# Streaming-encoder kernel: the head's transfers of x and of the first weight units in one queue, in order of use

## What is computed

```
def swiglu(x, w_gate, w_up, w_down):
    return (jax.nn.silu(x @ w_gate) * (x @ w_up)) @ w_down

for l in range(DEPTH):                       # DEPTH = 2
    h = rms_norm(x, ffn1_norm[l])
    x = x + 0.5 * swiglu(h, ffn1_w_gate[l], ffn1_w_up[l], ffn1_w_down[l])
    h = rms_norm(x, mix_norm[l])
    p = h @ w_in[l]
    ...                                      # attention, HGRN2, S5, all from p
    x = x + jnp.concatenate([o_a, o_b, o_c], axis=-1) @ w_out[l]
    h = rms_norm(x, ffn2_norm[l])
    x = x + 0.5 * swiglu(h, ffn2_w_gate[l], ffn2_w_up[l], ffn2_w_down[l])
```

## Time and profile before

| | us |
|---|---|
| median of three runs | 1030.37 |
| lowest and highest of them | 1029.40, 1030.59 |
| the profiled execution | 1029.56 |
| its span, first to last instruction | 1027.5 |
| PE busy in the span | 1014.0 (99%) |

### The profile page before, as it was taken

One profiled execution on the slowest core, in us unless ns is written; L12 is line 12 of the kernel. 1 busy time (PEld: TensorE's weight loads), 2 busy tenths in 40 slices (PEclk: granted clock), 3 DMA queues, 4 the chain that ended last, 5 costly groups with the idle time before them and its releaser, 6 DMA issues.

```text
span 1027.5 us, 20654 instructions
## 1 busy us (share of the span) xinstructions
PE 1014.0 (99%) x8562; PEld 946.8 (92%) x8562; DVE 744.4 (72%) x950; ACT 558.4 (54%) x699; POOL 199.2 (19%) x271
## 2 busy tenths in 40 slices
PE   9999999999999999999999999999999999999998
PEld 8998999999899999999999898989998998989898
DVE  7677778988778666565667777897987767666664
ACT  6656444655477645454476554446456866444442
POOL 0000899700002000000020019994000020000000
PEclk9999999999999999999999999999999999999999
DMA  8745354434325454645555455444442264554551
GB/s 302 277 151 217 151 211 157 165 127 162 125 83 205 164 209 160 209 158 210 187 193 207 173 195 202 166 147 181 142 149 84 86 243 166 204 187 181 187 180 41
DMA packets 26817, 178.39 MB, mean 174 GB/s; under 512 B 3120, under 2 KB 4160, under 8 KB 5760
## 3 DMA queue, kind: packets, MB, share of 16 engines
q1 hardware_dynamic: 25632, 173.03, 46.1%
q10 hardware_dynamic: 1008, 4.05, 1.1%
q0 software_dynamic: 112, 0.40, 0.1%
HBM read 176.42 MB, written 1.05 MB: 173 GB/s over the span
## 4 chain that ended last, share of the span: by engine, by line
PE 89%; DVE 7%; ACT 2%; issue 1%; DMA 0%; ACTq 0%; DVEq 0%
PE ps L887 23%; PE ps L835 16%; PE ps L836 16%; PE ps L837 16%; PE ps L889 12%; DVE lo L1246 2%; ACT hi L589 2%; PE ps L997 1%; PE ps L1106 1%; DVE fqk L1669 1%; PE ps L1050 1%; DMA x<-xT 0%; DVE in_lo L1484 0%; PE ps L1072 0%; DVE key L1550 0%
## 5 line engine op out<-in xcount | busy, mean ns | idle before, releaser
L887 PE MATMUL ps<-xg,hi 128*128 128x512 f32 x1120 | 397.8, 399 | 0.3
L1246 DVE TENSOR_TENSOR lo<-raw,hi 128x2048 fp32r<-128x2048 f32 x130 | 302.3, 2354 | 130.9 <-ACT hi L589 130.8
L889 PE MATMUL ps<-xg,lo 128*128 128x256 f32 x1120 | 315.0, 281 | 0.0
L589 ACT ACTIVATE hi<-raw 128x2048 fp32r<-128x2048 f32 x130 | 244.5, 1911 | 105.9 <-PE ps L889 82.5
L887 PEld LDWEIGHTS ps<-xg,hi 128*128 128x128 f32 x1120 | 210.7, 188 | 51.7 <-DVE lo L1246 0.9
L889 PEld LDWEIGHTS ps<-xg,lo 128*128 128x128 f32 x1120 | 212.0, 189 | 0.0
L835 PE MATMUL ps<-act_hi,hi 128*128 128x256 f32 x704 | 199.6, 284 | 0.6 <-DVE act_lo L1299 0.6
L836 PE MATMUL ps<-act_lo,hi 128*128 128x256 f32 x704 | 199.4, 283 | 0.0
L837 PE MATMUL ps<-act_hi,lo 128*128 128x256 f32 x704 | 199.4, 283 | 0.0
L835 PEld LDWEIGHTS ps<-act_hi,hi 128*128 128x128 f32 x704 | 134.9, 192 | 2.8 <-DVE lo L1246 0.8
L837 PEld LDWEIGHTS ps<-act_hi,lo 128*128 128x128 f32 x704 | 135.1, 192 | 0.0
(11 more groups left out here) (332 smaller groups left out, 1700.1 us busy)
## 6 DMA issues: line engine op xcount, KB each, us to landing
raw<-stream SPq DMA_DIRECT2D x160, 1024.0 KB, 4.9
par<-params ACTq DMA_DIRECT2D x2, 1463.0 KB, 8.2
raw<-stream SPq DMA_DIRECT2D x8, 256.0 KB, 7.1
rows<-stream SPq DMA_DIRECT2D x2, 1024.0 KB, 6.9
x<-xT ACTq DMA_DIRECT2D x4, 256.0 KB, 6.5
out<-x SPq DMA_DIRECT2D x8, 128.0 KB, 2.0
con<-consts POOLq DMA_DIRECT2D x1, 373.5 KB, 6.7
mask<-masks POOLq DMA_DIRECT2D x1, 20.0 KB, 6.5
```

The source lines that it names most:

```text
L589: e.activation(hi[slot][:, :], raw[slot][:, :], ACT.Copy).then_inc(hi_written, 1)
L887: pe.matmul(bank(b), hi[slot][:, w:w + P], xg[:, k, :, :].rearrange("p s t -> p (s t)"), start=k == 0, stop=False, skip_group_check=True)
L889: last = pe.matmul(bank(b)[:, 0:T], lo[slot][:, w:w + P], xg_hi[:, k, :], start=False, stop=k == KT - 1, skip_group_check=True)
L1246: v.tensor_tensor(lo[slot][:, :], raw[slot][:, :], hi[slot][:, :].bitcast(F32), ALU.subtract).then_inc(lo_written, 1)
```

## The change

1. SP issues x too: x tile 0, then the 256-column pieces of units 0 and 1 for that tile as one DMA; the same for tile 1; then pairs of tiles (2, 3), (4, 5), (6, 7). This is the new table FIRST. ACT issues only the gain.
2. ACT and DVE split in these five groups instead of four quarters. PE waits by them.
3. Unit 2 is issued in four quarters straight away, each with a semaphore, split in quarters by ACT and DVE, and multiplied by the new function `third_unit` tile by tile, with `row_sums` ahead of the last tile.
4. POOL's issue of the constants waits for group 3 (tiles 4 and 5), no longer for quarter 1 (tiles 2 and 3).
5. There are 12 matmuls on zeros, no longer 18.

```
+FIRST = [(0, 1), (1, 2), (2, 4), (4, 6), (6, 8)]
...
         @block.sync
-            for q in range(QUARTERS):
-                for s in range(2):
-                    c = slice(q * 512, (q + 1) * 512)
-                    sp.dma_start(raw[s][:, c], stream[s, :, c]).then_inc(first_loaded[q], 16)
+            for q, (at, end) in enumerate(FIRST):
+                sp.dma_start(x[:, at:end, :], xT[:, at:end, :]).then_inc(x_loaded[q], 16)
+                c = slice(at * 256, end * 256)
+                sp.dma_start(raw_all[:, 0:2, c], stream[0:2, :, c].rearrange("u p c -> p u c")
+                             ).then_inc(first_loaded[q], 16)
...
+            for q in range(QUARTERS):
+                c = slice(q * 512, (q + 1) * 512)
+                sp.dma_start(raw[2][:, c], stream[2, :, c]).then_inc(third_loaded[q] if q < QUARTERS - 1 else raw_loaded[2], 16)
...
-                load_split(l * SPLIT_UNITS + 2, l * UNITS + 2, 2)
+                if l:
+                    load_split(l * SPLIT_UNITS + 2, l * UNITS + 2, 2)
...
-            pool.wait_ge(first_loaded[1], 32)
+            pool.wait_ge(first_loaded[3], 16)
...
             e.dma_start(g0[:, :], gain0).then_inc(x_loaded[0], 16)
-            for q in range(QUARTERS):
-                e.dma_start(x[:, 2 * q:2 * q + 2, :], xT[:, 2 * q:2 * q + 2, :]).then_inc(x_loaded[q], 16)
...
-            split_hi(2, 0, 2)
+            for q in range(QUARTERS):
+                c = slice(q * 512, (q + 1) * 512)
+                if q < QUARTERS - 1:
+                    e.wait_ge(third_loaded[q], 16)
+                else:
+                    e.wait_ge(raw_loaded[2], 16)
+                e.activation(hi[2][:, c], raw[2][:, c], ACT.Copy
+                             ).then_inc(first_hi if q < QUARTERS - 1 else hi_written, 1)
...
+                def third_unit():
+
+                    for k in range(KT):
+                        if k == KT - 2:
+                            pe.wait_ge(lo_written, n0 + 3 + RING)
+                        elif k % 2 == 0:
+                            pe.wait_ge(first_lo, 2 * (len(FIRST) - 1) + k // 2 + 1)
+                        if k == KT - 1:
+                            row_sums(norm, False, 3)
+                        for m in range(2):
+                            w = k * 256 + m * P
+                            last = three(bank(6 + m)[:, 0:T], hi[2][:, w:w + P], lo[2][:, w:w + P],
+                                         xg_hi[:, k, :], xg_lo[:, k, :], k == 0, k == KT - 1)
+                    last.then_inc(units_done, 1)
...
-            for _ in range(18):
+            for _ in range(12):
                 pe.matmul(bank(0), zero[:, 0:P], zero[:, :], start=True, stop=True, skip_group_check=True)
```

65 lines of the change are left out of this document (38 added, 27 removed).

## The result

The changed kernel takes 1034.89 us, the median of six runs, where the kernel before takes 1030.43 on the same chip. The ratio is 1.0044, with a 95% interval of 1.0031 to 1.0058: slower by 0.44%, some 4.5 us. The forecast was 1028.7, with a range of 1026.0 to 1030.5. Both the size and the sign are wrong. One of the six executions took 1314.63 us at a mean PE clock of 0.695, and the ratio and its interval leave it out (the median of the other five is 1034.64).

The account below looks back on a forecast made before the run. PE's matmul chain was taken as the bound, leaving the head to win: PE 2.1 us earlier after unit 3, about 1.6 kept at the down projection, 1030.37 - 1.6 = 1028.8, stated as 1028.7; range 1026.0 to 1030.5.

Parts of the forecast that it names:

- (a) to (c): Head: gain landing, shorter pieces and twelve zeros put PE's first real matmul at 6.65, 2.05 us earlier than 8.69.
- (d): Feeding PE after its start: only group (2, 3) is late, ready at 9.95, so PE waits 0.45 us.
- inside the ranges: After 12 zeros, real work may begin at 1.2 GHz: half of such a stretch lost, less the 0.45 us wait.
- (e): Unit 2: the 0.25 us wait ahead of it goes; PE ends unit 3 at 30.45, 2.1 us earlier.
- (c): Zeros: twelve instead of 18 end at 6.6, so PE's first real matmul comes at 6.65.
- (f): Down projection's other condition: unit 4 lands at 21.5, down projection starts at 31.1, so about 1.6 of 2.1 us remain.
- Nothing is won: Rival, chance 0.09: unit 4 lands at 23.05 as before, logarithm at 26.29, time 1030.4.
- The small pieces are slow: Rival, chance 0.07: head transfers with 1 KB rows stay at 137 GB/s through group (2, 3), time 1034.4.
- A clock stretch moves: Rival, chance 0.17: slow clock stretches behind mixer holes go; 1027.0 if one goes, 1025.3 if both.

Follow-up runs that it names:

- e5: Changed kernel with pairs of tiles in place of the single tiles, against the kernel before: 1.0005.
- e12: Repeat of the changed kernel with pairs of tiles in place of the single tiles, against the kernel before: 1.0014.
- e7: Kernel before with only unit 2's part of the change (issued and split in quarters, multiplied tile by tile): 1.0006.
- e9: Changed kernel with pairs, `row_sums` ahead of tile 5 and unit 4 split behind the exponential, against the kernel before: 1.0013.
- e14: The changed kernel run again unaltered, against the kernel before: 1.0047.
- e13: Changed kernel with six matmuls on zeros of 16 columns added behind the twelve of 512, against the kernel before: 1.0019.
- e6: Changed kernel with 18 matmuls on zeros instead of 12, against the kernel before: 1.0018.
- e10: Changed kernel with four single tiles ahead of two pairs, against the kernel before: 1.0023.
- e3: Changed kernel with x on ACT's queue and each two-unit piece issued as two transfers, against the kernel before: 1.0068.
- e8: Kernel before with 12 matmuls on zeros instead of 18, against the kernel before: 1.0020.
- e2: Changed kernel with each two-unit piece issued as two transfers, one a unit, x still on SP, against the kernel before: 1.0024.

## Why the prediction was wrong, step by step

**What bounds the kernel: right, and it was not used far enough.** That a microsecond ahead of 8.69 "is worth one only if it is still there at 32.70" was the right test. The start was won, and it wasn't there. In the other direction 18 zeros lost 1.4 us of the start and won 2.7 in all.

**(a) to (c), PE's start at 6.65: right.** It was 6.75, and 6.08 in the repetition. The gain landed earlier than I had it, about 3.4 for 4.66, and ACT began at 3.41. As the zeros end at 6.75 anyway, this gave nothing. That PE then follows the zeros without a gap, and that 1.94 for 2.05 us are won there, came true.

**(d), PE fed: this is the step that failed.** I had group (2, 3) landed at 8.0, ready at 9.95, and a wait of 0.45. Measured: 10.4, 12.53 and 2.75. The sum took a group as landed when the queue's bytes up to it are through, and took the rates from the trace of before, 349 and then 328 GB/s. The rates were indeed lower, 292 and 246, but from 1.5 to 3.5 us more passed than before (204 for 137), and with all three measured rates the 1577 KB are through at 8.0 and landed at 8.6. That is 0.6 of the 2.4 us. The larger part is the other assumption: the 16 DMA engines do not stay abreast. By the completions in the trace ten engines had brought their share of the weights between 7.80 and 8.24, close to the forecast, and gone on to later groups; the other six finished between 9.35 and 10.40, and the group is complete with the last. My sum had no term for this, and no row of before showed it: there the engines lie within 1.2 us of each other up to unit 2.

What makes it late is the singles, and that is shown by experiment. With the groups alone changed to pairs it is early, at 8.5 (e5) and 8.1 (e12). In the eight profiles of kernels that begin with singles, the changed one and its repetition among them, the group landed at 9.1 to 12.5; in the nine without singles whose transfers fill all partitions, the kernel before among them, at 7.8 to 8.8: the two sets do not overlap. With pairs alone the change is slower than before by 0.05% in one series and 0.14% in the other, instead of 0.44% and 0.47%: some 3 to 4 us better. *Why* singles do this is open. The engines that fell behind (six in the changed kernel, four in its repetition, three with 18 zeros) stay behind until unit 2's quarters have landed. Neither the shared queue nor the pieces of two units is the reason by itself, and doubling the singles did not double the lag. Since the pairs show a lag too, from the same place in the queue but one group later, the singles may do no more than bring it forward to a group for which PE has nothing in hand; that it goes by the number of transfers ahead, and not by their size, is not tested. The trial by half transfers, made for this question, failed for a cause of its own.

**The cost "inside the ranges" was the one that left them.** I did think of the 1.2 GHz level, but behind the zeros, where it did not come, and I priced it at half a microsecond against a wait of 0.45. It came behind the hole that step (d) left. Between the zeros and unit 2 the longest hole was 1.6 us or less in ten executions, and no slow stretch followed; it was 2.1 us or more in seven, and one followed each time. Elsewhere shorter holes had it too: with four singles one came at 34.7, behind a hole of 1.78 ahead of the down projection, and holes of 1.8 to 2.0 near 184 us and in the mixer had it in some executions and not in others. So a late landing can cost PE its hole and another 1.6 us. The arithmetic of the head closes: the work behind the hole is placed as if PE had started at 12.53 - 2.88 = 9.65, which is 0.96 later than before, plus 1.6 of slow clock, less 0.25 for the hole ahead of unit 2: 2.3, measured 2.21.

**(e), unit 2: right.** Its wait of 0.25 is gone, in the changed kernel and in e7, where the edit alone is worth nothing that can be measured (1.0006). Only the times in it are wrong with (d).

**(c) again: a cost of taking instructions away.** All nine kernels with twelve zeros and nothing in the place of the other six, as far as their profile can be read, have the issue hole of 0.6 to 0.9 us among the narrow matmuls at 264 to 270 us; none of the seven with 18 matmuls there has it, the kernel before among them. That it comes from the *number* of instructions is shown by the narrow ones, which bring it back to none in both kernels. It was no term of my sum, and no row of before could have given it.

**(f), the other condition: half right.** The chain from unit 4's split to `act_lo` did decide. But unit 4 was not there at 21.5: it landed at 25.7. Without singles, and with transfers that fill all partitions, it lands at 22.5 to 23.6 in nine kernels, whatever the head does, and in eight of them the first DMA engine brings it 1.5 to 1.7 us ahead of the last (0.5 in the ninth). "Nothing is won", with 0.09, had this right, and it would have capped the gain had (d) held: pairs with a start 0.45 ahead of before end at 32.78, as before. Taking the logarithm off this condition (e9) won 0.5 at the down projection and nothing in the time, as the same splits then stand behind it.

**The rivals.** "The small pieces are slow" named the right place and the right side, at 1034.4 for 1034.89, but its number is luck. Its mechanism was a low rate, at which it decides from a mean of 212 GB/s down. The mean from 1.5 to 9.75 us was 247, by which nothing would have been lost. What made the group late was the engines' lag, and that gives 0.96 at group (2, 3), not 4; the clock and the issue hole made up the rest. The Trainium skill (DMA: Bandwidth & Descriptors, Bandwidth) had counselled large transfers; by that rule the edit goes the wrong way, and the times now agree in sign. The experiments do not follow the size, though: with one unit a transfer, smaller ones still, the ratio was 1.0024, and with four singles 1.0023, both better than the change. "A clock stretch moves" had one go in the profiled execution (784 us), but another grew, and one came in the head. Of the Trainium skill's sentence (TensorE: Matmul & The Clock Gate, Part 1) that the point of the change varies from run to run, the trace shows this much: changed kernel and repetition have the mixer's stretches at 279.8 only, and at 281.7 and 790.3.

**What the 4.5 us are, by medians.** The zeros edit: 1.0044 and 1.0047 against 1.0018, some 2.7 to 3.0 us; in the profiles the slow clock in the head is 1.6 of it and the issue hole 0.8. The rest, 0.18% or 1.9 us, is the late landing itself: with 18 zeros the down projection starts at 34.59, 1.9 behind the kernel before, and with pairs at 32.78. The gain of 1.94 at the start is in neither, since PE with an earlier start only waits longer for the same tiles. How much of the 2.7 is the clock and how much the issue hole was not parted by a run of its own.

The mean granted clock of every execution is on record, however, and it says more than the profiles. As PE is busy 98% of the time, 0.001 of the mean clock is worth about 1.0 us (estimate: 0.001 of 1033 us); the executions of the kernel before bear this out, with 1032.24 us in mean at 0.995 and 1028.97 at 0.998 in the third series. Averages over the executions that a ratio uses, the kernel before beside it, and what the difference is worth by that estimate:

| kernel | clock | before | worth, us | measured, us |
|---|---|---|---|---|
| changed again (e14) | 0.9930 | 0.9962 | 3.3 | 4.6 |
| 12 and 6 narrow (e13) | 0.9952 | 0.9962 | 1.0 | 2.0 |
| 18 zeros (e6) | 0.9971 | 0.9972 | 0.1 | 1.6 |
| four singles (e10) | 0.9963 | 0.9964 | 0.1 | 2.1 |
| both undone (e3) | 0.9945 | 0.9977 | 3.3 | 6.0 |
| before, 12 zeros (e8) | 0.9955 | 0.9972 | 1.8 | 2.1 |

A slow stretch of 3.4 us lowers the mean by 0.0017. So the changed kernel has on average nearly two such stretches more than the kernel before, not only the one in the head, and the slow clock is the largest part of its loss. The second is behind the first in one profile (e14, 6.8 us from 12.1) and in the mixer in the other. Between e13 and e14, side by side, 2.3 of the 2.6 us go by the clock. Why six narrow matmuls spare the second stretch is open, and these estimates don't add up with the issue hole and the late landing to the tenth.

## What to carry to other kernels

An earlier start is worth what the *second* and third group allow: forecast when each next group lands before the start is counted, and not by bytes and rate alone: here the last DMA engine was 2.6 us behind the first. Filler work that lasted until the data were there cost nothing here, and taking it away can cost more than it frees, since the hole that it leaves may bring the clock down. When the number of instructions changes ahead of a tightly fed part, look for a wait on issue in a place that the edit never touched.

## What was not expected of the hardware

- Two single tiles ahead (128 KB of x, 256 KB of weights each, rows of 1 KB a partition) put the landing of the *next* group, of the same size and shape, from 7.8 to 8.8 us to 9.1 to 12.5, with the DMA engines 80% busy instead of 94% in between (5 to 9 us). The bytes kept flowing (247 GB/s in mean); some engines fell behind and the group waited for them. The cause inside the queues is open.
- Transfers that write 64 of the 128 partitions ran at 236 to 242 GB/s with all DMA engines busy; with all partitions, where no singles went ahead, 298 to 421.
- Six matmuls of 16 columns on zeros took 0.83 us, nearly as much as two of 512 (0.43 each in that place). Each has a weight load of 128 columns of its own, which the narrow ones of the mixer (32 columns) have not, so the two kinds can't be compared.
- PE stood 0.6 to 0.9 us for its own instructions in the middle of 64 matmuls of 16 columns, where 54 of these take 0.65 us. The page of the changed kernel has 46 transfers of instructions, with the columns number, MB and share of 16 engines' span; one of 16 KB ran from 265.64 to 266.61 us, and PE, idle from 266.96, went on at 267.83, 1.2 us after its end. In four other kernels with the hole (e2, e8, e12, e14) PE went on 1.2 to 1.4 us after the end of such a transfer. Six instructions fewer ahead make this wait appear, and six narrow ones take it away. That such a transfer is what PE waited for is an inference from these times; that the number of instructions decides is shown.

```profile
q8 instruction: 46, 0.75, 0.3%
```
